# Hybrid attention and convolution layer: the low parts of the last stage's weights stored once and loaded by four of the five blocks

## The reference

```python
def finish_layer(h, att, cv, p, w_out, g_ffn, w_gate_up, w_down, g_ple, w_ple_gate, w_ple_proj):
    h = h + jnp.concatenate([att, cv], axis=-1) @ w_out
    u = rms_norm(h, g_ffn)
    gate, up = jnp.split(u @ w_gate_up, 2, axis=-1)
    h = h + (jax.nn.silu(gate) * up) @ w_down
    g = jax.nn.sigmoid(rms_norm(h, g_ple) @ w_ple_gate)
    return h + g * (p @ w_ple_proj)
```

## Time and profile before

| | |
|---|---|
| Median of 3 runs | 2917.2 us (2913.88 to 2917.88) |
| Profiled execution | 2914.39 us, span 2912.6 us, granted TensorE clock 0.984 |
| TensorE matmul / weight load | 94% / 90% busy, 14844 each |
| VectorE | 73% busy, 2923 instructions |
| ScalarE | 40% busy, 1895 |
| GpSimd | 49% busy, 726; 379 of them on L1626, 1023.4 us |
| DMA | 136 GB/s over the span, 331.70 MB read and 65.07 MB written |

### The profile page before, as it was taken

The page is one execution under the profiler, slowest core; times in us unless marked ns, Lnnn a source line. Parts: engine busy times, 40 slices in busy tenths (PEclk is TensorE's granted clock), DMA queues, the critical chain, the costliest instruction groups (busy, mean ns, idle before and its releaser), DMA issues.

```text
span 2912.6 us, 38961 instructions
## 1 busy us (share of the span) xinstructions
PE 2747.1 (94%) x14844; PEld 2629.8 (90%) x14844; DVE 2137.6 (73%) x2923; ACT 1153.6 (40%) x1895; POOL 1418.2 (49%) x726
## 2 busy tenths in 40 slices
PE   7999989999979899998999998999988989999998
PEld 6888979999968899998899998999988988999998
DVE  4555458877748888678988678987788987774565
ACT  5333347667644223342233442233432223432333
POOL 5111227777734455444555444555444544455554
PEclk9999989999989999999999999999999999999999
DMA  4444585665432343342333432433433323433333
GB/s 157 166 141 162 166 293 167 206 207 154 142 127 101 105 142 120 113 160 101 122 125 121 140 132 98 142 116 114 150 108 101 131 101 107 150 110 122 110 123 102
DMA packets 184613, 397.29 MB, mean 136 GB/s; under 512 B 22092, under 2 KB 123084, under 8 KB 183884
## 3 DMA queue, kind: packets, MB, share of 16 engines
q1 hardware_dynamic: 184428, 394.80, 40.6%
HBM read 331.70 MB, written 65.07 MB: 136 GB/s over the span
## 4 chain that ended last, share of the span: by engine, by line
PE 43%; DVE 23%; ACT 4%; issue 1%; POOL 1%; DVEq 0%; ACTq 0%
PE c_acc L160 42%; DVE y L1674 10%; DVE c_hid L1749 5%; DVE wres L1752 2%; DVE c_g L1743 1%; ACT wres L1599 1%; DVE c_g L1738 1%; ACT c_sig L1595 1%; DVE c_up L1746 1%; ACT wres L1529 1%; DVE c_rstd L1700 1%; POOL wres L1626 1%; ACT L1546 0%; DVE ul L1690 0%; DVE wres L1659 0%
## 5 line engine op out<-in xcount | busy, mean ns | idle before, releaser
L1626 POOL TENSOR_TENSOR wres<-x,wres 128x1024 fp32r<-128x1024 f32 (+2 forms) x379 | 1023.4, 2700 | 1047.1 <-ACT wres L1529 1047.1
L160 PE MATMUL c_acc<-uh,wres 128*128 128x416 f32 x4160 | 1161.4, 356 | 66.4 <-POOL wres L1626 65.6
L160 PEld LDWEIGHTS c_acc<-uh,wres 128*128 128x128 f32 x4160 | 783.3, 189 | 96.7 <-POOL wres L1626 83.9
L1529 ACT ACTIVATE wres<-x 128x1024 fp32r<-128x1024 f32 (+2 forms) x379 | 434.4, 1146 | 806.1 <-PE c_acc L160 806.1
L160 PE MATMUL c_acc<-ul,wres 128*128 128x416 f32 x2080 | 730.3, 351 | 0.0
L160 PE MATMUL c_acc<-wres 128*128 128x416 f32 x3600 | 693.0, 353 | 30.9 <-POOL wres L1626 18.8
L160 PEld LDWEIGHTS c_acc<-wres 128*128 128x128 f32 x3600 | 674.3, 189 | 48.7 <-POOL wres L1626 23.6
L1674 DVE SCALAR_TENSOR_TENSOR y<-c_gw,vec,y 128x416 f32<-128x416 f32 (+1 forms) x600 | 504.4, 903 | 0.0
L160 PEld LDWEIGHTS c_acc<-ul,wres 128*128 128x128 f32 x2080 | 393.8, 189 | 7.5 <-issue 1.6
L160 PE MATMUL a_acc<-uh,wres 128*128 128x416 f32 x1088 | 318.2, 363 | 13.1 <-POOL wres L521 9.2
L1690 DVE SCALAR_TENSOR_TENSOR ul<-z,vec,uh 128x416 fp32r<-128x416 f32 x80 | 180.6, 2263 | 80.1 <-ACT uh L1533 80.1
(11 more groups left out here) (171 smaller groups left out, 3156.4 us busy)
## 6 DMA issues: line engine op xcount, KB each, us to landing
x<-in_w_gu SPq DMA_DIRECT2D x220, 512.0 KB, 3.2
x<-in_w_down SPq DMA_DIRECT2D x80, 704.0 KB, 4.0
x<-in_w_ple SPq DMA_DIRECT2D x40, 640.0 KB, 3.9
x<-in_w_in SPq DMA_DIRECT2D x40, 512.0 KB, 3.9
x<-in_w_out SPq DMA_DIRECT2D x40, 512.0 KB, 3.7
z<-in_x SPq DMA_DIRECT2D x57, 208.0 KB, 4.4
v_d<-a_v SPq DMA_DIRECT2D x20, 416.0 KB
qh_d<-a_room SPq DMA_DIRECT2D x40, 208.0 KB, 2.3
```

The lines of the kernel that those rows point to most:

```text
L160: mm = nc.tensor.matmul(out, w[wp](kw), u[up](ku), start=first and n == 0 and j == 0, stop=last and n == len(kts) - 1 and j == 2)
L1529: nc.scalar.activation(whi[v % 2][:, 0:kts, :], raw[v % 2][:, 0:kts, :], ACT.Copy).then_inc(hi_done, 1)
L1626: nc.gpsimd.tensor_tensor(wlo[v % 2][:, 0:kts, :], raw[v % 2][:, 0:kts, :], whi[v % 2][:, 0:kts, :].bitcast(F32), ALU.subtract).then_inc(l ...
```

## The change

- **finish, block 0**: the low parts are made on GpSimd as before, now in four buffers, and SyncE stores each into a tensor in the chip's memory (`low_store`). **Blocks 1 to 4**: GpSimd does nothing; SyncE loads the stored low part beside the raw weights (`low_load`), and TensorE waits for the high part and for that load.
- ScalarE takes the high part of the hidden tile f - 1 in the G unit f, behind the weights' high part, not in the U unit; VectorE's low part of it follows it there. Only the last tile of a half keeps its place.
- P units do the gate's 24 matmuls first and the p product's 6 after them, with its wait between (unit 0 keeps its order). Y units wait for the convolution's tiles one by one. The sum of block 0's convolution squares comes after unit 0 in place of unit 1.
- **project**: three rooms for raw weights in the first block in place of two (the third lies in the part of `rstd` that later blocks write), loads issued accordingly; `sum_x`, its root and its reciprocal come one unit later. **attend** gets new semaphore counts only.
- Semaphores of the weights are shared by the stages, and buffers move inside `wres`.

```diff
+            "w_out": dram("w_out_lo", (D, D), F32), "w_gu": dram("w_gu_lo", (2 * FF, D), F32),
+            "w_down": dram("w_down_lo", (D, FF), F32), "w_ple": dram("w_ple_lo", (D, D + PLE), F32),
...
-    c["f_lo"] = [tiles(flat, first, half, P) for first in (18432, 21248)]
+    c["f_lo"] = [tiles(flat, first, half, P) for first in (18432, 14848, 21248, 22656)]
...
-        w_raw = room[:, :, :].rearrange("p s (k c) -> p s k c", c=P)
+        later = rstd[:, 2:, :].rearrange("p b n -> p (b n)")[:, 0:KD * P]
+        w_raw = [e.rearrange("p (k c) -> p k c", c=P) for e in (room[:, 0, :], room[:, 1, :], later)]
...
-                m = i if i < QK else QK + i - V0
-                sp.dma_start(room[:, i % 2, :], t["w_in"][m * P:(m + 1) * P, :]).then_inc(w_in[i % 2], 16)
+                if i >= 3:
+                    sp.wait_ge(lo_done, i - 2)
+                sp.dma_start(w_raw[i % 3].rearrange("p k c -> p (k c)"),
+                             t["w_in"][i * P:(i + 1) * P, :]).then_inc(w_in[i % 3], 16)
...
-            weights(1)
-            for i in range(2, 4):
-                sp.wait_ge(lo_done, i - 1)
+            for i in range(1, 3):
                 weights(i)
             for bi, i in units:
-                if bi == 0 and i + 4 < NU:
-                    sp.wait_ge(lo_done, i + 3)
-                    weights(i + 4)
+                if bi == 0 and i + 3 < NU:
+                    weights(i + 3)
                     sp.wait_ge(x_lo, KD * (bi + 1))
+                    if bi == 0:
+                        for q in range(2):
+                            sp.wait_ge(sq_first[q], KD // 2)
...
+                if bi == 2:
+                    act.wait_ge(lo_done, NU)
...
-                if i == 7 and bi + 1 < NB:
+                if i == 8 and bi + 1 < NB:
                     sqrt_rs(bi + 1)
...
-                if i == 6 and bi + 1 < NB:
+                if i == 7 and bi + 1 < NB:
                     sum_x(bi + 1)
...
-                if v >= 4:
-                    sp.wait_ge(lo_done, v - 2)
+                if v >= 3:
+                    if units[v - 2]["b"] == 0:
+                        sp.wait_ge(lo_done, L0 + split[v - 2])
+                    else:
+                        sp.wait_ge(hi_done, H0 + v - 2)
+                sp.dma_start(unit_tiles(raw[v % 2], u, u["kts"]), unit_rows(t, u)).then_inc(w_in[v % 2], 16)
+
+            def low_store(v):
+                u = units[v]
+                if v:
+                    sp.wait_ge(lo_done, L0 + split[v])
+                sp.dma_start(unit_rows(s, u), unit_tiles(wlo[v % 4], u, u["kts"]).bitcast(F32)).then_inc(low_dma[v % 4], 16)
+
+            def low_load(v):
+                u = units[v]
+                sp.wait_ge(used, U0 + v - 3)
+                sp.wait_ge(low_dma[v % 4], 16 * (v // 4))
+                sp.dma_start(unit_tiles(wlo[v % 4], u, u["kts"]).bitcast(F32), unit_rows(s, u)).then_inc(low_dma[v % 4], 16)
...
             weights(2)
+            low_store(0)
             for m in range(4):
                 x_load(0, m)
-            sp.wait_ge(lo_done, 1)
             weights(3)
+            low_store(1)
...
                 if v + 4 < NU:
                     weights(v + 4)
+                    if units[v + 4]["b"]:
+                        low_load(v + 4)
+                if v + 2 < NU and units[v + 2]["b"] == 0:
+                    low_store(v + 2)
...
+            def hidden_high(b, half, f):
+                n = f_count(b, half, f)
+                act.wait_ge(hid_out, n + 1)
+                nc.scalar.activation(hh(f), hid[:, :], ACT.Copy).then_inc(hid_hi, 1)
...
                 elif kind == "G":
-                    if u["half"] == 0 and u["f"] == 0:
+                    if u["f"]:
+                        hidden_high(b, u["half"], u["f"] - 1)
+                    elif u["half"] == 0:
                         norm(b, 0)
                     act.wait_ge(left, u["left0"] + 1)
                     nc.scalar.activation(sig[:, :], g[:, :], ACT.Sigmoid).then_inc(sig_out, 1)
                 elif kind == "U":
-                    n, f = f_count(b, u["half"], u["f"]), u["f"]
-                    act.wait_ge(hid_out, n + 1)
-                    nc.scalar.activation(hh(f), hid[:, :], ACT.Copy).then_inc(hid_hi, 1)
+                    if u["f"] == HF - 1:
+                        hidden_high(b, u["half"], u["f"])
...
-                if v:
-                    pool.wait_ge(hi_done, v)
-                    nc.gpsimd.tensor_tensor(wlo[v % 2][:, 0:kts, :], raw[v % 2][:, 0:kts, :],
+                if v and u["b"] == 0:
+                    pool.wait_ge(hi_done, H0 + v)
+                    if v >= 4:
+                        pool.wait_ge(low_dma[v % 4], low_count(v - 4))
+                    nc.gpsimd.tensor_tensor(wlo[v % 4][:, 0:kts, :], raw[v % 2][:, 0:kts, :],
                                             whi[v % 2][:, 0:kts, :].bitcast(F32), ALU.subtract).then_inc(lo_done, 1)
...
+                    if u["f"]:
+                        hidden_low(b, u["half"], u["f"] - 1)
                     dve.wait_ge(sig_out, sig_count(b, "G", u["half"] * HF + u["f"] + 1))
                     dve.wait_ge(left, u["left0"] + 1)
                     nc.vector.tensor_tensor(g[:, :], g[:, :], sig[:, :], ALU.mult).then_inc(gs_out, 1)
...
-                    dve.wait_ge(hid_hi, n + 1)
-                    nc.vector.tensor_tensor(hl(f), hid[:, :], hh(f).bitcast(F32), ALU.subtract).then_inc(hid_lo, 1)
+                    if f == HF - 1:
+                        hidden_low(b, u["half"], f)
...
-                w = [lambda k: whi[v % 2][:, k, :], lambda k: wlo[v % 2][:, k, :]]
+                w = [lambda k: whi[v % 2][:, k, :], lambda k: wlo[v % 4][:, k, :]]
                 out = acc[:, u["banks"][0], 0:N]
-                if v:
-                    pe.wait_ge(lo_done, v)
+                if v == 0:
+                    pe.wait_ge(c["first_split"], 2)
+                elif b == 0:
+                    pe.wait_ge(lo_done, L0 + split[v])
                 else:
-                    pe.wait_ge(c["first_split"], 2)
+                    pe.wait_ge(hi_done, H0 + v)
+                    pe.wait_ge(low_dma[v % 4], low_count(v))
...
-                    if kind == "Y":
-                        pe.wait_ge(cv_lo, (b + 1) * CT)
                     for e in range(2):
-                        mm = passes(nc, acc[:, u["banks"][e], 0:N], w, M, [(CT * e + k, half + k) for k in range(CT)],
-                                    kind == "X", kind == "Y")
+                        for k in range(CT):
+                            if kind == "Y" and e == 0:
+                                pe.wait_ge(cv_lo, b * CT + k + 1)
+                            mm = passes(nc, acc[:, u["banks"][e], 0:N], w, M, [(CT * e + k, half + k)],
+                                        kind == "X" and k == 0, kind == "Y" and k == CT - 1)
...
-                    if b or m >= 2:
-                        pe.wait_ge(e_out, b * KD + max(m - 1, 0))
-                    passes(nc, acc[:, 4 + m % 2, 0:N], w, E, [(KD + k, k) for k in range(KP)], True, True)
+                    if b and m < 2:
+                        pe.wait_ge(e_out, b * KD)
                     if m == 0:
+                        passes(nc, acc[:, 4, 0:N], w, E, [(KD + k, k) for k in range(KP)], True, True)
...
                     else:
-                        mm = passes(nc, out, w, U, [(k, k) for k in range(KD)], True, True)
+                        passes(nc, out, w, U, [(k, k) for k in range(KD)], True, True)
+                        if m >= 2:
+                            pe.wait_ge(e_out, b * KD + m - 1)
+                        mm = passes(nc, acc[:, 4 + m % 2, 0:N], w, E, [(KD + k, k) for k in range(KP)], True, True)
...
-                if v == 1:
+                if v == 0:
```

129 lines of the change are left out of this document (72 added, 57 removed).

## The result

The changed kernel takes 2795.0 us (median of four runs, 2791.39 to 2795.48). On the same chip the kernel before takes 2916.7. The ratio is 0.9581, 95% interval 0.9565 to 0.9598: 4.2% faster. The time lies inside the range of 2755 to 2803, 22 us above the forecast of 2773. The profiled execution took 2795.48 us, its span 2793.8, at a mean granted clock of 0.988.

The account below looks back on a forecast made before the run. Finish was taken as TensorE's, with a 150.5 us surcharge caused by other engines. Blocks 1 to 4 (104.6), block 0 (25) and project (14) sum to 144 us off 2914.4; plus 2.8 for the median, 2773 us, range 2755 to 2803.

Parts of the forecast that it names:

- Blocks 1 to 4: Finish without GpSimd's subtractions: TensorE's surcharge of 111.8 us goes, less 4 x 1.8, a gain of 104.6 us.
- The stall at P2: Third P unit of each finish block: 1.1 us of idle stays, 1.3 with the slow first matmuls.
- No wait of VectorE's stands ahead of it: Block 0, ScalarE's high part in the new order: both halves reach the second half's state, 16.7 us gained.
- the first D units: Block 0 of finish: of 2.9 us lost at the first D unit of a half, 0.8 stays; 2.1 counted.
- the start: Block 0 of finish: the squares' sum moves to after unit 0, so unit 2 and all behind start 4.6 us earlier.
- The rival: "Block 0 stays slow": VectorE falls behind until ScalarE waits, pairs back at 10.6 us, 17 us lost, 2790; chance 0.12.
- A third room lets the loads go one unit ahead: Project's first block: ScalarE's wait for tile 6 goes and what stands behind comes 5.0 us earlier.
- the two other terms: Project, `sum_x` one unit later: 4.3 us at the first block's unit 8, 4.5 in the blocks after.
- stay: Attend and the stages' changeovers were to keep their time, a change of 0.
- project gains nothing: Project, or the start, brings no gain: 2773 + 5 to 14, about 2785 us; chance 0.10.
- The clock: Rival in finish: the clock falls when TensorE never pauses, granted 0.95, 96 us more, 2869; chance 0.03.
- The slower case: Rival in blocks 1 to 4: the DMA rate is the bound, at 200 GB/s 474 us a block, 3135; chance 0.04.

Follow-up runs that it names:

- e3: The changed kernel with the hidden tile's high and low part back in its U unit, low parts still stored and loaded: 2803.7 us, ratio 0.9609.
- e4: The changed kernel with one more unread 512 KB load behind each low load in blocks 1 to 4: 2857.0 us, ratio 0.9782.
- e1: The changed kernel with project's raw weight loads issued one SyncE iteration earlier, still three rooms: 2783.0 us, ratio 0.9533.
- e5: e1 with ScalarE's square root of the gate's norm ahead of the weights' high part in finish: 2771.4 us, ratio 0.9493.
- e8: e1 with the sum of x back at unit 6, its root and reciprocal back at 7: 2785.3 us, ratio 0.9545.

## Why the prediction was right or wrong, point by point

- **Blocks 1 to 4: right in mechanism and size**, 104.9 us for 104.6. No GpSimd after block 0, L1812 (L1749 before) at a mean of 0.59 us, 247 to 251 GB/s for the 246 worked out (229 in block 4). The stall at P2 is there, 1.23 us on L1835 for the 1.1 worked out. e3 and e4 show why it holds: the order isn't needed there, and the engines can move a third more than these loads ask for. No wait of TensorE's in these blocks names a load of low parts.
- **Block 0: the step "No wait of VectorE's stands ahead of it" failed.** The sigmoid waits for VectorE, and the high part of the next iteration stands behind the sigmoid. The first half went from 117.2 to 105.9 us where 100.5 was worked out (-11.3 for -16.7); the first D units gained 0.1 us for 2.1; the start gained 5.2 for 4.6, the P units 1.0 for 1.3; the second half's units lost 0.6. The rival was right that VectorE falls behind and ScalarE waits for it, but the pair is 9.48 us and not 10.6, so in the first half it costs a third of what that rival said. Its budget of 9.33 us in a pair of 9.07 counted 2.83 us for a subtraction that was itself being held; with 2.40 the work fits, at 8.9. The second half does hold 9.07 us with the same work: the engines stand in another phase there, and what puts them into it I haven't found.
- **Project: the step "A third room lets the loads go one unit ahead" failed.** A free room doesn't send a load. The load stood in SyncE's list behind the cache piece of the iteration before, and that wait is VectorE's. I had counted the loads and not what each is queued behind. Of the two other terms, the sum's place in blocks 1 to 3 came out at 2.7, 1.5 and 1.1 us for 2.8, 1.3 and 0.4; unit 8 in the first block started 1.6 us earlier, not 9. With the loads put on time (e1) attend starts 12.6 us earlier than in the trace before, 15 by the means: about the 14 worked out.
- **Attend: "stay" was too firm.** It takes 430.5 us before and 429.9 to 437.8 in the eleven other kernels, whose work there is the same. The profiled execution of the changed kernel has the longest. That makes 7.3 of the 24.7 us between the forecast for the profiled execution (2770.8) and its 2795.48, beside 9.8 of project and 7.9 of block 0. A band of some 4 us either way belonged into the range for it.
- **The rivals.** Block 0 as a whole came out 7.9 us over, half-way to "stays slow" (2790), and "project gains nothing" (2785) was true but for some 3 us. Both happened together, which the upper end of 2803 had allowed for. The clock didn't fall where TensorE never pauses: 1.00 over each block of finish. The one stretch at the lower level there, a granted clock of 0.57 from 860 to 864 us, follows the wait of 4.4 us for GpSimd in block 0. The slower case is ruled out by the changed kernel itself, which moves 247 to 251 GB/s over blocks of 385 us. The range held because it was wide enough for two of the small losses together; attend's 7.3 us were in none of its terms.

## What to carry to other kernels

A buffer more gives a lead only if the transfer is also issued earlier: for every load, write down what stands ahead of it in its queue, and what that waits for. Where VectorE and GpSimd both work on SBUF, add up the two for one period of the loop, with times of instructions that weren't held, and compare with the period. Where the sum nearly fills the period, as 8.9 of 9.07 us did here, the order of the engines can decide whether it fits (11.1 us in block 0 between e3 and the changed kernel); taking the work off one of them helps in any order. Before an activation of another kind on ScalarE, look for its table load: it can run while ScalarE waits anyway, if no other work stands ahead of it.

## What the runs showed of the hardware

**What the DMA engines moved with this mix.** Mostly loads of 512 to 704 KB into SBUF, all on one queue, beside a TensorE that was busy for 97% of the time (e4): 338 GB/s at a share of 0.92 to 0.93 over 800 us, 387 over 40 us.

**VectorE beside GpSimd.** A tap on 128x416 with two SBUF inputs takes 0.64 us alone and 2.44 on average when it overlaps a subtraction of GpSimd's; an eviction from PSUM takes 0.58 us either way (e5).

**Attend's length differs between executions of the same code.** Windows of attend, of the changed kernel, of e8 and of e1:

```profile
406.00:843.80 437.80, 414.87 (x2824) 395.63 (x2825) 331.44 (x932) 284.66 (x717) 297.95 (x277) 0.94 0.56 178
```

```profile
403.50:833.40 429.90, 411.18 (x2825) 392.45 (x2825) 330.56 (x932) 284.84 (x717) 298.35 (x277) 0.95 0.56 181
```

```profile
397.60:831.70 434.10, 409.89 (x2825) 391.03 (x2825) 331.52 (x932) 284.76 (x717) 297.73 (x277) 0.96 0.56 180
```

Of the 7.9 us between the first two 3.7 are TensorE's busy time, at a mean granted clock of 0.94 against 0.95: TensorE pauses for up to 3.3 us about every 100 us there, and stretches at the lower of its two clocks (1.2 in place of 2.4 GHz) come with the pauses, with lengths that differ: from 525.8 to 536.0 us in the changed kernel, behind a pause of 1.9 us, and from 521.7 to 525.1 in e8. The other 4.2 are idle time. The clock alone doesn't explain the length: e1 has the highest mean clock of the three (0.96) and the least busy time (409.9 us), and still takes 434.1. What sets the idle time is open; no run here was made for it. Attend sets the limit for what a total can tell: e8 and e1 differ by 5.9 us in project and by 2.2 in the medians.
